# 25 modulation units on VectorE instead of 22, later turns at the first down product, and other PSUM banks behind norms

## The reference

```
mod = (silu(c) @ mod_w[i] + mod_b[i]).reshape(B, 3, 3, D)     # one row of 9216 numbers for each layer i
shift, scale, gate = mod[:, :, 0], mod[:, :, 1], mod[:, :, 2]
h = modulate(rms_norm(x, norm_g[i, 0]), shift[:, 0], scale[:, 0])
x = x + 0.5 * gate[:, 0] * swiglu(h, w_gate[i, 0], w_up[i, 0], w_down[i, 0])
h = modulate(rms_norm(x, norm_g[i, 1]), shift[:, 1], scale[:, 1])
y = fox_attention(h, ...) if i == 0 else dilated_attention(h, ...)
x = x + gate[:, 1] * y
h = modulate(rms_norm(x, norm_g[i, 2]), shift[:, 2], scale[:, 2])
x = x + 0.5 * gate[:, 2] * swiglu(h, w_gate[i, 1], w_up[i, 1], w_down[i, 1])
```

## Time and profile before

| | |
|---|---|
| median of 3 runs | 2241.78 us (2241.42 to 2245.81) |
| the profiled execution | 2246.45 us, its span 2244.8 us |
| TensorE busy | 2149.6 us, 96% of the span |
| VectorE, ScalarE, GpSimd busy | 66%, 48%, 7% |
| mean granted clock of TensorE | 0.987 of full speed |
| read from HBM | 445.40 MB, 199 GB/s over the span |

### The profile page before, as it was taken

How to read it: one execution, slowest core, us unless ns; L and a number is a source line. 1 busy time by engine, 2 the same in 40 slices (tenths; PEclk the granted TensorE clock), 3 DMA queues, 4 the chain that set the end, 5 groups by cost and what they waited for, 6 DMA issues and landing times.

```text
span 2244.8 us, 33167 instructions
## 1 busy us (share of the span) xinstructions
PE 2149.6 (96%) x14132; PEld 1892.1 (84%) x14132; DVE 1484.3 (66%) x1939; ACT 1084.6 (48%) x1220; POOL 147.5 (7%) x180
## 2 busy tenths in 40 slices
PE   7999898999999999899999999999999999999998
PEld 5998665998799778687799887897998878988996
DVE  4677666776677666666665455567786655677874
ACT  4443465443444344645544335644555357435552
POOL 0311110111011100000000011000000110000000
PEclk9999999999999999999999999999999999999999
DMA  9977662977687756245275565534655564436551
GB/s 346 300 274 252 251 230 76 299 262 262 202 279 271 245 206 215 86 156 182 87 230 179 197 224 169 169 123 165 208 182 196 177 222 132 169 136 220 178 180 55
DMA packets 264259, 448.62 MB, mean 200 GB/s; under 512 B 11520, under 2 KB 147008, under 8 KB 263856
## 3 DMA queue, kind: packets, MB, share of 16 engines
q1 hardware_dynamic: 246784, 382.93, 51.5%
q0 software_dynamic: 17040, 62.46, 7.7%
q10 hardware_dynamic: 288, 1.11, 0.1%
HBM read 445.40 MB, written 1.06 MB: 199 GB/s over the span
## 4 chain that ended last, share of the span: by engine, by line
PE 87%; ACT 5%; DVE 5%; issue 1%; DMA 1%; POOL 0%; SPq 0%; ACTq 0%; DVEq 0%; POOLq 0%
PE ps L1494 85%; DVE wlo L1924 2%; ACT whi L1719 2%; PE ps L1685 1%; PE ps L1652 1%; ACT S L1719 1%; ACT L1719 1%; ACT xs L1719 1%; ACT xhi L1719 0%; DMA raw<-in_fox_w_in 0%; DMA raw<-in_mod_w 0%; PE ps L1642 0%; DVE S L2072 0%; DVE x L1974 0%; PE ps L1602 0%
## 5 line engine op out<-in xcount | busy, mean ns | idle before, releaser
L1924 DVE TENSOR_TENSOR wlo<-raw,whi 128x2048 fp32r<-128x2048 f32 (+1 forms) x339 | 769.6, 2278 | 402.8 <-ACT whi L1719 402.6
L1719 ACT ACTIVATE whi<-raw 128x2048 fp32r<-128x2048 f32 (+1 forms) x339 | 640.9, 1895 | 389.8 <-PE ps L1494 361.3
L1494 PE MATMUL ps<-xhi,whi 128*128 128x256 f32 x2632 | 650.5, 287 | 8.1 <-DVE wlo L1924 3.5
L1494 PE MATMUL ps<-xhi,wlo 128*128 128x256 f32 x2632 | 644.7, 285 | 0.0
L1494 PEld LDWEIGHTS ps<-xhi,whi 128*128 128x128 f32 x2632 | 508.8, 193 | 14.2 <-issue 4.8
L1494 PEld LDWEIGHTS ps<-xhi,wlo 128*128 128x128 f32 x2632 | 509.1, 193 | 1.8 <-issue 1.4
L1494 PE MATMUL ps<-xlo,whi 128*128 128x256 f32 x2632 | 344.3, 283 | 0.1
L1494 PEld LDWEIGHTS ps<-xlo,whi 128*128 128x128 f32 x2632 | 327.6, 192 | 0.5 <-DVE xlo L2038 0.3
L1494 PE MATMUL ps<-whi,xhi 128*128 128x512 f32 x736 | 297.1, 404 | 18.2 <-ACT xhi L1719 11.2
L1494 PE MATMUL ps<-wlo,xhi 128*128 128x512 f32 x736 | 291.3, 396 | 0.0
L1494 PE MATMUL ps<-whi,hhi 128*128 128x512 f32 x528 | 211.3, 400 | 5.7 <-DVE hlo L2048 4.1
(11 more groups left out here) (233 smaller groups left out, 1942.0 us busy)
## 6 DMA issues: line engine op xcount, KB each, us to landing
raw<-in_w_in SPq DMA_DIRECT2D x52, 1024.0 KB, 5.1
raw<-in_ffn_w_gate SPq DMA_DIRECT2D x88, 512.0 KB, 4.7
raw<-in_ffn_w_up SPq DMA_DIRECT2D x88, 512.0 KB, 5.9
raw<-in_ffn_w_down SPq DMA_DIRECT2D x44, 1024.0 KB, 5.0
raw<-in_w_up SPq DMA_DIRECT2D x88, 512.0 KB, 4.9
raw<-in_dil_w_in SPq DMA_DIRECT2D x36, 1024.0 KB, 5.2
raw<-in_mod_w SPq DMA_DIRECT2D x28, 1024.0 KB, 7.0
nbuf<-in_mod_w POOLq DMA_DIRECT2D x44, 512.0 KB, 5.2
```

Source lines behind the costliest of these rows:

```text
L1494: return nc.tensor.matmul(o, lhs, rhs, start=start, stop=stop, skip_group_check=True)
L1719: return nc.scalar.activation(o, i, func, **kw)
L1924: V.tensor_tensor(wlo[:, s["c"], 0:s["n"]], raw[:, s["slot"], 0:s["n"]], whi[:, s["c"], 0:s["n"]].bitcast(F32), ALU.subtract).then_inc(sem ...
```

## The change

Three more of the 36 units are made by VectorE: 9, 8, 8 and 0 units in the four FFNs, for 7, 7, 7 and 1 (units 4 to 12 of layer 0 in FFN (0,0)). Other units stand at the norms, two instead of four lie in the forgetting attention and none in the dilated one. VectorE gets a third accumulator, in the other half of `xs`. In FFN (0,0) a gateup takes 2 and 3 parts instead of 2 and 2. At the first down product the counts of finished units are not lowered, so that a turn which isn't due yet comes behind that product. Behind a norm with the x transposes in G0, G1, D0 and D1 the units take D2/D3, G0/G1, G2/G3 instead of D2/D3, G2/G3, G0/G1.

```diff
-        self.acc_free = [None, None]
+        self.acc_free = [None] * 3
...
+        self.work_turn, self.work_rate = 0, (2, 2)
...
-    def run_turns(self, mod_only=False):
+    def run_turns(self, mod_only=False, age=True):
...
-        for entry in self.acc_turns:
+        for entry in self.acc_turns if age else ():
             entry[0] -= 1
         while self.acc_turns and self.acc_turns[0][0] < 0:
             self.acc_turns.pop(0)[1]()
 
-    def run_work(self, n=2):
-
+    def run_work(self, n=None):
+
+        n, self.work_turn = n or self.work_rate[self.work_turn], 1 - self.work_turn
         for _ in range(min(n, len(self.work)) if self.work_on else 0):
             self.work.pop(0)()
...
-        acc = self.n_units % 2
+        acc = self.n_units % 3
...
     def begin_units(self):
 
-        self.pair = 0
-        self.first_pair = (D2, D3) if self.turn_banks[0] == G0 else None
+        self.pair = int(self.turn_banks[0] == G0)
+        self.first_pair = (D2, D3) if self.pair else None
...
         if q == 0:
-            self.run_turns()
+            self.run_turns(age=False)
             self.in_down = True
...
-        plan.run_work(len(plan.work))
+        plan.run_work(len(plan.work) + 1)
...
-        in_norm = {("ffn", 0, 1): (0, 16), ("ffn", 1, 0): (1, 6), ("ffn", 1, 1): (1, 16), ("mix", 0): (0, 11), ("mix", 1): (1, 14)}
-        on_vector = {(0, 0): [(0, u) for u in range(4, 11)], (0, 1): [(0, 17)] + [(1, u) for u in range(6)],
-                     (1, 0): [(1, u) for u in range(7, 14)], (1, 1): [(1, 17)]}
-        fill = {0: [(0, u) for u in range(12, 16)], 1: [(1, 15)]}
+        in_norm = {("ffn", 0, 1): (1, 6), ("ffn", 1, 0): (1, 7), ("ffn", 1, 1): (1, 17), ("mix", 0): (0, 13), ("mix", 1): (1, 16)}
+        on_vector = {(0, 0): [(0, u) for u in range(4, 13)], (0, 1): [(0, 16), (0, 17)] + [(1, u) for u in range(6)],
+                     (1, 0): [(1, u) for u in range(8, 16)], (1, 1): []}
+        fill = {0: [(0, 14), (0, 15)], 1: []}
...
-                        for m in fl[:2 if r == 1 else 1] if hh == 0 else ():
+                        for m in fl[:1] if hh == 0 and r else ():
...
-                self.work_on = True
+                self.work_on, self.work_rate = True, (2, 3) if (i, s["j"]) == (0, 0) else (2, 2)
...
-        macc = [mod_rows[:, 1, :], xs[:, 1, 0:512]]
+        macc = [mod_rows[:, 1, :], xs[:, 1, 0:512], xs[:, 1, 512:D]]
```

## The result

The changed kernel took 2249.73 us in the median of 10 runs (2246.20 to 2252.70), the kernel before 2245.09 us beside it (2240.05 to 2246.56). The ratio is 1.0024, with a 95% interval of 1.0014 to 1.0035: slower by about a quarter of a per cent. I had forecast 2229 us and gave 0.84 to faster. The ratio applied to the 2241.78 us that the forecast started from gives 2247.2, so the forecast was wrong by about 18 us (by 20.7 against the median beside it), and it lies outside the range of 2218 to 2239.

A forecast was written before the change was run, and what follows sets the result against it. TensorE, busy 2149.6 of 2244.8 us, was taken to bound the kernel. The terms -4.6 - 3.4 - 4.8 - 5.2 - 4.4 + 9.6 = -12.8 us took the median from 2241.78 to 2229 us, range 2218 to 2239.

The forecast's parts named there:

- (a): Three units move from TensorE to VectorE: 4.6 us less; eight more parts in the first FFN's gateups stay hidden.
- three pieces ahead: VectorE converts weights three pieces ahead of their use, so no wait for a conversion was expected.
- if VectorE's queue rather than TensorE's paces the gateups: In the first FFN: one of the signs named beforehand that would show the forecast wrong.
- (b): Forgetting attention: TensorE's two waits of 1.40 and 2.02 us around modulation units go, 3.4 us less.
- One sign that I had named: Forgetting attention, changed profile: no idle of ScalarE over 3 us for fox weights.
- (c): Own banks at norms: all four TensorE waits for a bank to be emptied go, 4.8 us less.
- (d): First down products of three FFNs: without hastening the gaps go, except 0.5 us in the first FFN; 5.2 us less.
- (e): TensorE's clock drops behind the gaps at 167.6, 532.1 and 822.3 go with those gaps, 4.4 us less.
- (f): End of the first FFN: TensorE waits 7.9 us for the ninth unit, plus 1.7 us of clock; 9.6 us more.
- The slower one: Rival: the ninth unit's four loads ahead of the tail meet a crowd, gap of 27 us, 2248 us; chance 0.06.

The follow-up runs named there:

- experiment 3: Changed kernel with seven units in FFN (0,0), plus one VectorE operation of a part's size per gateup that waits for no load: 2229.49 us, ratio 0.9938.
- Experiments 1: Changed kernel with FFN (0,0) as before (seven VectorE units, 2 and 2 parts a gateup), all else kept: 2227.41 us, ratio 0.9934.
- experiment 6: Changed kernel with a third place for the loads of VectorE's parts, every part where it was: 2230.39 us, ratio 0.9948.
- experiment 7: Changed kernel with 3 and 3 parts a gateup in FFN (0,0): two load places 2241.50 us, ratio 0.9995; three places 2226.15 us, ratio 0.9922.
- experiment 4: Changed kernel, FFN (0,0): 3 and 2 parts instead of 2 and 3, ratio 1.0033; or fifth part behind the hidden product, ratio 0.9986.
- experiment 8: Three places, 3 and 3 parts: every VectorE unit turned one gateup later, ratio 0.9931; or no such turn in FFN (0,0)'s last gateup, ratio 0.9893.

## Why the prediction was wrong

**(a), the step that failed.** I wrote of the eight more parts in the gateups: "hidden, since weights are converted ahead". I had counted their 6 us of work against VectorE's idle time in a window, and the work is indeed hidden (experiment 3). I had not asked when the load of each part is issued and when it is due, and put the wait for it at nothing. I worked that out for the tail, load by load, and not for the gateups, where the same two places serve five parts for four. The cover that I named was also thinner than "three pieces ahead": VectorE can't convert what ScalarE hasn't copied, and ScalarE's copies stand behind `hhi`, which waits for the product behind the waiting part. Experiments 1, 6 and 7 show the loads' places as the cause. The cost inside FFN (0,0) was 25.9 us where my terms there come to 8.2 (two turns 1.6, -1.3 and -1.7 at the first down product, +9.6 at the tail). The 17.7 us between them took the whole gain, and the third place alone gave 17 back. I had named the sign of it ("if VectorE's queue rather than TensorE's paces the gateups") but gave it no price and no chance.

**(b) Right at the waits, and too small.** Both waits of the earlier trace rows are gone. One sign that I had named is missing all the same: ScalarE still idles 6.52 us for a fox weight, up to 301.89 (before it was 8.29 and 7.40 us), but TensorE has no gap over 0.5 us there. The attention gained 11.2 us; my terms there were 3.4, two units' matmuls and turns (2 x 2.34 = 4.7) and the 0.78 of (c) at its norm, 8.9 in all. The other 2.3 us lie in two rows that I had not read: a wait for `nm` (L2064) in the attention fell from 1.85 us (at 352.69) to 0.35 (at 367.12), and the wait for `xs` at the norm behind it from 1.89 to 0.90. Nothing here shows that the change caused either; the second also stands at 0.90 in the run with own banks alone.

**(c) Right.** No gap over 0.5 us behind any norm's first unit; alone it gave 4.5 us (forecast 4.8 and some clock).

**(d) Right at two of three places.** At FFN (0,1) and (1,0) the gaps of 1.66 and 2.27 us are gone. The edit alone gave 8.7 us; by my terms for these gaps and their clock (5.75 and 3.0) it is 8.8. For FFN (0,0) I left 0.5 us because the column would have "no product and no `hlo` ahead of it". It had four parts, a conversion and one wait for a load (2.50 us) ahead of it, from the turn at 171.18 to the column at 179.45, and cost 7.68. With the loads in time (experiment 6) it was 0.41, so the 0.5 holds on a condition that I did not state.

**(e) Partly.** The clock at these places is 1.00, but new gaps bring new drops in FFN (0,0), 7.6 us in all, and one place drops without a new gap (below).

**(f) The gap right, 7.89 for 7.9; the clock behind it mis-sized.** VectorE waits there for two loads, 1.00 and 3.45 us, and they took 4.7 and 5.7 us for the 4.7 that I took. At half clock and its return TensorE lost about 3.0 us for the 1.7 that I took. The gap begins at 236.6 and not at 222.3, since all ahead of it was late.

**A count that I had wrong.** I wrote that six loads move onto GpSimd's queue. It is twelve: three units of four loads, and GpSimd's row on the page goes from x180 to x192. The six are those of `nbuf` alone. No term of the sum used it.

**The rivals.** The slower one had the right sign and the wrong place: I put the late loads in a crowd ahead of the tail and priced it at a gap of 21 us or more. No load there was that late. Small waits in eight gateups, handed on by two queues, did it.

By the Trainium skill, DMA: Bandwidth & Descriptors, Anatomy of one DMA (2.0 us and the bytes at 436 GB/s), such a load takes an estimated 3.2 us. The one above took 6.3 us, and from 72 to 168 us the changed kernel's nbuf loads took 4.4 to 7.4:

```profile
DMA to landing us min/median/max: 4.4/6.2/7.4
```

By 3.2 us the load issued at 144.62 would be there at 147.8, just ahead of its part. The trace does not agree.

**What stays open.** How much of (b)'s extra gain is fewer weights in the stream and how much is luck of one profiled execution; whether a wait for a load costs less in the first slot of a gateup than ahead of the product, since no run moved all of them there; the load waits were not split into queueing and transfer; and the extra work of experiment 3 was not tried in the other three stages.

## What to carry to other kernels

When work with its own transfers is made denser, hold each transfer's issue against the time at which it is due, place by place: with two places a load had 10.8 us at four parts a gateup and 3.4 us at five. Idle time of the engine doesn't answer this, for an in-order queue that waits holds back all that stands behind it, and the engines that wait for that. Here another place gave 0.76% and 0.73% (experiments 6 and 7), and dealing the same parts out to other slots between nothing and 0.4% (experiment 4). A turn into a bank that a stage is about to claim goes behind that stage's first step also when it is due, where the engine that empties the bank has much work ahead of it (0.3% here, experiment 8).

## What the hardware showed that I had not expected

The granted clock is not set by the gap alone. In the second block both kernels wait 2.24 us for the same conversion, up to 1435.46 before and up to 1433.95 in the changed kernel. The window behind it, before and then changed:

```profile
1434.00:1438.00 4.00, 2.54 (x11) 2.12 (x12) 3.97 (x8) 2.68 (x2) 0.00 (x0) 1.00 0.30 79
```

```profile
1434.00:1438.00 4.00, 4.00 (x11) 3.14 (x12) 3.93 (x11) 1.17 (x1) 0.00 (x0) 0.61 0.73 234
```

One stayed at 2.4 GHz (1.00 from 1438 to 1442 too), the other was in part at 1.2. Of the 14 kernels traced twelve have such a drop behind this same wait (2.23 to 2.26 us); only the kernel before and the one without hastening alone have none. In FFN (0,0) smaller gaps did both as well: 1.82 us before with a drop to 0.57, 1.33 us in the kernel of experiment 7 with two places with none (1.00 from 120 to 124). The gaps of 3.81 us (at 169.65 in experiment 7 with three places, 0.63 from 170 to 174) and more were each followed by a drop.
